# Small projections of the front half on column groups of TensorE, summed and turned by products with an identity

## The reference, cut to what matters

```python
uc = modulate(xc, norm_pre_mix[l], csh1, csc1) @ w_in[l]     # context tokens
u  = modulate(x,  norm_pre_mix[l], sh1,  sc1)  @ w_in[l]     # latent tokens
...
ba = u[..., GDN_CONV_CH + GDN_V:]        # 32 columns: beta and g of the first mixer
beta = jax.nn.sigmoid(ba[:2])
g = -jnp.exp(A_log)[:, None, :, None] * jax.nn.softplus(ba[2:] + dt_bias[:, None, :, None])
...
dt_raw = u[..., SSD_CONV_CH + SSD_INNER:]   # 16 columns: dt of the second mixer
dt = jax.nn.softplus(dt_raw + dt_bias.reshape(2, 1, G, Hg, 1))
```

## Time and profile before

| | us |
|---|---|
| median of 3 runs | 1415.59 |
| lowest and highest | 1414.0, 1417.88 |
| the profiled execution's own time | 1415.84 |
| its span | 1414.0 |
| TensorE busy | 1259.0 (89%) |
| VectorE busy | 485.5 (34%) |
| ScalarE busy | 254.6 (18%) |
| moved by DMA | 458.59 MB, 324 GB/s on average |

### The profile page before, as it was taken

How to read it: one execution, slowest core, us unless ns; L and a number is a source line. 1 busy time by engine, 2 the same in 40 slices (tenths; PEclk the granted TensorE clock), 3 DMA queues, 4 the chain that set the end, 5 groups by cost and what they waited for, 6 DMA issues and landing times.

```text
span 1414.0 us, 25289 instructions
## 1 busy us (share of the span) xinstructions
PE 1259.0 (89%) x10245; PEld 576.8 (41%) x10246; DVE 485.5 (34%) x1026; ACT 254.6 (18%) x494; POOL 122.9 (9%) x169
## 2 busy tenths in 40 slices
PE   5999898657997999998889988887999999999995
PEld 2545355556754334333333333332333334333432
DVE  1155369735767213221232212311223213212223
ACT  2321442235122111111111111000000100100101
POOL 0201460164300000000000000000000000000000
PEclk8999999658997999999999999998999999999998
DMA  9859111010494999999999999999999699969993
GB/s 355 330 169 360 35 60 44 4 33 4 136 346 184 425 429 425 427 426 428 427 426 428 425 428 426 427 426 426 427 427 420 264 426 428 426 266 428 427 427 145
DMA packets 48134, 458.59 MB, mean 324 GB/s; under 512 B 4416, under 2 KB 4816, under 8 KB 22736
## 3 DMA queue, kind: packets, MB, share of 16 engines
q1 hardware_dynamic: 48080, 457.81, 78.3%
HBM read 456.15 MB, written 1.05 MB: 323 GB/s over the span
## 4 chain that ended last, share of the span: by engine, by line
PE 59%; DMA 30%; DVE 5%; issue 3%; ACT 2%; POOL 1%; DVEq 0%; SPq 0%; ACTq 0%; POOLq 0%
DMA arena<-in_w_up 29%; PE bank L1154 22%; PE bank L1183 9%; PE bank L667 7%; PE bank L1125 3%; PE bank L1116 2%; PE bank L583 2%; PE bank L1047 2%; PE bank L543 2%; DVE arena L1726 1%; ACT arena L1541 1%; PE bank L592 1%; DMA arena<-in_x 1%; PE bank L1147 1%; PE bank L896 1%
## 5 line engine op out<-in xcount | busy, mean ns | idle before, releaser
L1154 PE MATMUL bank<-arena 128*64 128x512 f32 x2176 | 482.0, 596 | 35.2 <-DMA arena<-in_w_up 19.6
L1154 PEld LDWEIGHTS bank<-arena 128*64 128x64 f32 x2176 | 155.3, 136 | 342.9 <-issue 267.0
L1183 PE MATMUL bank<-arena 128*64 128x512 f32 x1088 | 239.4, 592 | 0.0
L2253 DVE TENSOR_SCALAR arena<-bank 128x512 f32<-128x512 f32 x34 | 23.6, 693 | 392.7 <-PE bank L1154 392.7
L1183 PEld LDWEIGHTS bank<-arena 128*64 128x64 f32 x1088 | 78.9, 136 | 137.7 <-issue 135.4
L667 PE MATMUL bank<-arena 128*128 128x512 f32 (+1 forms) x320 | 125.2, 545 | 0.0
L2234 DVE TENSOR_TENSOR arena<-arena,bank 128x512 f32<-128x512 f32 x140 | 86.7, 683 | 6.0 <-PE bank L1125 6.0
L667 PEld LDWEIGHTS bank<-arena 128*128 128x128 f32 x320 | 61.4, 196 | 59.0 <-issue 56.0
L1116 PEld LDWEIGHTS bank<-arena 128*128 128x128 bf16 x1680 | 60.2, 118 | 27.0 <-DVE arena L2257 25.8
L1125 PE MATMUL bank<-arena 64*128 64x512 f32 x280 | 69.6, 614 | 0.9 <-ACT arena L1543 0.9
L1543 ACT ACTIVATE arena<-bank 128x512 f32<-128x512 f32 x34 | 20.3, 598 | 253.2 <-PE bank L1183 253.2
(11 more groups left out here) (346 smaller groups left out, 1081.8 us busy)
## 6 DMA issues: line engine op xcount, KB each, us to landing
arena<-in_w_gate SPq DMA_DIRECT2D x64, 2048.0 KB, 20.3
arena<-in_w_up SPq DMA_DIRECT2D x64, 2048.0 KB, 21.9
arena<-in_w_down SPq DMA_DIRECT2D x64, 2048.0 KB, 20.6
arena<-in_w_ada SPq DMA_DIRECT2D x12, 2048.0 KB, 9.6
arena<-in_wfm SPq DMA_DIRECT2D x20, 512.0 KB, 3.4
arena<-in_wz SPq DMA_DIRECT2D x4, 1024.0 KB, 13.8
arena<-in_w_out SPq DMA_DIRECT2D x2, 2048.0 KB, 8.9
arena<-in_x SPq DMA_DIRECT2D x2, 1024.0 KB, 7.6
```

The lines of the kernel that those rows point to most:

```text
L1154: last = mm(ps[m][64 * c_:64 * c_ + 64, :], xcT[:, k, :], ring[:, 2 * h_ + m, k % 4, 512 * c_:512 * c_ + 512], start=False, stop=(k == KT ...
L1183: last = mm(ps[2][64 * c_:64 * c_ + 64, :], hidT[:, k % 4, 64 * (k // 4):64 * (k // 4) + 64], ring[:, 4 + h_, k % 4, 512 * c_:512 * c_ + 5 ...
L2253: v.tensor_scalar(hid[:, 0], ps[0][:, :], LIMIT, None, ALU.min).then_inc(*L.mark("a"))
```

## The change

The six `small_of` calls go. In their place stand two pieces.

`small_products()`, in one place behind `z_of(1, 1, 1)`, makes the weights the stationary operand. Part 0 takes 32 of the 48 columns over tokens 0 to 511, part 1 takes columns 16 to 47 over the context and the permuted latent tokens. Feature block `k` stands in column group `k % 4`, so a bank (2 for part 0, 3 for part 1) holds four partial sums with the weight columns on the partitions and 512 tokens in the row. ScalarE copies each bank to `smT`, which lies where `xh` was.

`small_sums()`, behind `fm(0)`, takes 128 tokens of `smT` as the stationary operand and `eye32` (an identity of 32 stacked four times over the partitions) as the moving one. One product sums the four groups and turns the result to tokens on partitions. `eye32` is made by GpSimd, as before.

`cumulate()` moves from behind `fm(1)` to behind `fm(2)`, and VectorE's reading of it from block 1 to block 2.

```diff
+        smT = view(area("xh"), 2, 512)
...
-            def small_of(t, lo, hi):
-
-                base = t * 128 if lo == 0 else 512 + (t - 2) * 128
-                for k in range(KT):
-                    last = mm(smp[:, t, lo:hi], xmT[:, k, base:base + 128], wsmt[:, k, lo:hi],
-                              start=(k == 0), stop=(k == KT - 1))
+            def small_products():
+
+                pe.wait_ge(*L.at("in", "wsm", 1))
+                for t in range(2):
+                    pe.wait_ge(*L.at("act", "xmT", t))
+                    pe.wait_ge(*L.at("dve", "xmT", t))
+                for part in range(2):
+                    for k in range(KT):
+                        g = k % 4
+                        dst = view(ps[2 + part][32 * g:32 * g + 32, :], 2, 256)
+                        tokens = xmT[:, k, 0:768].rearrange("p (a b) -> p a b", a=3)[:, 0:3:2, :] if part else view(xmT[:, k, 0:512], 2, 256)
+                        last = mm(dst, wsmt[:, k, 16 * part:16 * part + 32], tokens, start=k < 4, stop=k >= 4)
+                    last.then_inc(*L.mark("smT", part))
+
+            def small_sums():
+
+                pe.wait_ge(*L.at("pool", "eye32"))
+                pe.wait_ge(*L.at("act", "smT", 1))
+                for t in range(NT):
+                    mm(smp[:, t, 0:32], smT[:, 0, 128 * t:128 * t + 128], eye32, start=True, stop=True)
+                    last = mm(smp[:, t, 32:48], smT[:, 1, 128 * t:128 * t + 128], eye32[:, 16:32], start=True, stop=True)
                 last.then_inc(*L.mark("sm"))
...
             z_of(0, 1, 1)
             rows_turned(0)
-            pe.wait_ge(*L.at("in", "wsm", 1))
-            small_of(2, 0, 32)
             z_of(1, 0, 1)
             rows_turned(1)
-            small_of(3, 0, 32)
-            pe.wait_ge(*L.at("act", "xmT", 0))
-            pe.wait_ge(*L.at("dve", "xmT", 0))
-            small_of(0, 0, 48)
             z_of(1, 1, 1)
-            pe.wait_ge(*L.at("act", "xmT", 1))
-            pe.wait_ge(*L.at("dve", "xmT", 1))
-            small_of(1, 0, 48)
-            small_of(2, 32, 48)
-            small_of(3, 32, 48)
+            small_products()
...
                 if i < NFM:
                     fm(i)
-                if i == 1:
+                if i == 0:
+                    small_sums()
+                if i == 2:
                     cumulate()
...
             z_out(1, 1)
+            for part in range(2):
+                act.wait_ge(*L.at("pe", "smT", part))
+                f(smT[:, part], ps[2 + part][:, :], ACT.Copy).then_inc(*L.mark("smT", part))
...
-                if i == 1:
+                if i == 2:
                     dve.wait_ge(*L.at("pe", "cum"))
```

## The result

| | before | after |
|---|---|---|
| median of four runs | 1416.74 us (1414.0 to 1419.05) | 1400.99 us (1398.16 to 1402.47) |
| profiled execution | 1415.84 us, span 1414.0 | 1402.24 us, span 1400.4 |
| granted clock of TensorE | 0.954 | 0.960 |

The two profiled executions differ by 13.6 us, of which the forecast covers 6.6. The question is where the other 7 us come from.

What follows compares the result with a forecast made beforehand. The prediction took TensorE alone to bound the front, from 55.95 us to the `row` product. 10.48 + 1.70 - 3.71 - 0.15 - 1.71 = 6.6 us off 1415.84 gave 1409.2 us, range 1405.8 to 1413.3.

Steps and rivals of the forecast that it cites:

- The small products, 3.71 us: Ahead of `fm(0)`: the 16 added column-group products take 2 x 1.855 = 3.71 us, by the `ada_chunk` row.
- The sums, 1.71: Behind `fm(0)`: the eight added products of `small_sums` take 1.71 us, with ScalarE's second copy to `smT` hidden.
- Leaving the groups, 0.15: At `fm(0)`, now behind column groups: leaving them adds 0.15 us, as for `fm(2)` behind an `ada_chunk`.
- Full overlap: In `small_products`: four column groups overlap as in `ada_chunk`, eight products in 1.86 us (3.8 times).
- Side engines, cover 0.2 us: At the `row` product: VectorE's `mod` is ready at 94.0 us, the product due at 94.2, leaving 0.2 us.
- rival (b): At the `row` product: it waits for VectorE's `mod`, stretched convolutions costing 0.5 or 1.1 us; 1410.3 us, chance 0.10.
- The clock, 1.70 us: First two `fm` blocks: without the narrow products TensorE's clock no longer falls, so 1.70 us come back.
- Rival (a): Around `fm`: the clock gain isn't had, as it falls anyway or not all earlier runs fell; 1.70 us, 1410.9, chance 0.14.
- Every microsecond taken from TensorE there moves all that follows: From 55.95 us to the `row` product: the chain is TensorE alone, so savings carry through unless another engine becomes late.
- the result line 1415.84 - 6.6: Whole kernel: the profiled execution's 1415.84 us less the front's 6.6 us gives 1409.2 us.
- Rival (c): Beyond the front: the gain is given back at a stage started by something not moved; 1415.6 us, chance 0.07.

Runs made afterwards that it cites:

- the kernel before at place 0: Kernel before plus 161 semaphore increments on TensorE that nothing waits for, spread over the `fm` products: 1410.51 us, ratio 0.9981 against the kernel before.
- the changed kernel at place 95: Changed kernel plus 95 semaphore increments on TensorE that nothing waits for, spread over the `fm` products: 1405.86 us, ratio 0.9951 against the kernel before.
- two later measurements: Changed kernel word for word, 1402.27 us, and with 256 semaphore increments more on TensorE, 1402.93 us; ratios 0.9909 and 0.9928 against the kernel before.
- its repeat: Changed kernel measured once more, word for word, against more runs of the kernel before: 1402.27 us, ratio 0.9909.
- the sums early: Changed kernel with `small_sums` directly behind `small_products`, ahead of `fm(0)`: 1411.41 us in one run.
- the changed kernel with 32 fillers: Changed kernel plus 32 semaphore increments on TensorE that nothing waits for, spread over the `fm` products: median 1406.24 us, ratio 0.9945 against the kernel before.
- the kernel before with its narrow products apart: Kernel before with the last two `small_of` calls (16 columns) moved behind `fm(0)` and `cumulate` behind `fm(2)`: 1422.66 us in one run.

## Why the prediction was wrong, by its steps

- **The small products, 3.71 us**: 3.57. **The sums, 1.71**: 1.69, with ScalarE's copy hidden. **Leaving the groups, 0.15**: the block behind `small_products` takes 7.07 us, one behind the sums 6.96. The z products, which the prediction left at 3.52 and 3.51, took 3.44 each.
- **Full overlap**: 3.9 times, measured. The rule that was set against it (the Trainium skill, TensorE: Matmul & The Clock Gate, Part 3, three groups at 0.79 of the ideal), taken over to four groups, doesn't hold for these products.
- **Side engines, cover 0.2 us**: a wait of 0.24 us at the `row` product, by the slow first step of the second convolution, which overlaps a GpSimd product that starts at 89.55 us: a small form of rival (b), within the profile's 6.61 us. That the front gave 6.61 us to the hundredth is luck in part: this wait was made up by the z products and the 0.14 us of the small ones.
- **The clock, 1.70 us**: the mechanism was right, and the size was right for the execution it was read from. The prediction took the 3.51 us and 4.38 us stretches as harmless because one execution had passed them; two other executions fell behind such a stretch. Rival (a) feared that not all runs have the fall; all four profiles with this order of narrow products have one, and one of them has two. How much more than 1.70 us that makes on average is not shown.
- **"Every microsecond taken from TensorE there moves all that follows"**, and the result line 1415.84 - 6.6: this is the step that failed. It takes the later stages as fixed in length. They depend on where TensorE's breaks fall, and the change shifts those by 95 instructions. Worth about 3 us: the first stretch takes 22.4 to 23.4 us at the old place and 18.6 to 20.9 at the new one, in both kernels, and the medians say 2.6 (the kernel before at place 0) and 3.8 to 4.7 (the changed kernel at place 95). Rival (c) asked only whether something gives the gain back, never whether something adds to it.
- **The size that was measured**: 6.6 and 3 are 9.6 us, and the two later measurements gave 11.1 and 12.0, each uncertain by some 4 us; both of their medians are still below the range. The 15.8 us of the first had four runs of either kernel, of kernels whose single runs spread over 18 (before) and 11 to 15 us (changed). Even the 1415.84 us that the forecast started from is some 2 us above the medians of the kernel before in the later comparisons. In the first pair of profiles the 7 us beyond the front are 3.8 of the first stretch (23.44 against 19.62), less the 1.3 of the later start; most of the rest, 2.7 us, lies between 323 and 350 us of the kernel before, where the other executions don't follow the place. The spread sits between the load of `x` and that of `w_out`: 65.1 us in the changed kernel's profile and 71.1 in its repeat, where the granted clock from 280 to 350 us was 0.79 and 0.70. The repeat has some 24 us on end at the low clock there; three of the other 14 profiles have the like (the sums early, the changed kernel with 32 fillers, and the kernel before with its narrow products apart; 1411.41, 1413.47 and 1422.66 us). So it comes with either front. These are the two rows:

```profile
280.00:350.00 70.00, 51.22 (x2032) 44.85 (x2027) 34.01 (x65) 34.06 (x96) 48.84 (x50) 0.79 0.08 23
```

```profile
280.00:350.00 70.00, 51.74 (x1818) 43.57 (x1815) 30.18 (x58) 31.17 (x91) 46.52 (x47) 0.70 0.05 18
```

Open are three things: what a break is, since only its period and its effect were measured; what brings on the long low clock between 330 and 375 us in some executions; and what brings the clock down behind one narrow stretch of 3.5 us and not behind the next.

## What to carry to other kernels

Replace products that stream few columns by products in column groups: here that saves the work and, with it, clock falls of which one profile may show only a part. If a change alters the number of TensorE's instructions, expect stretches of tiny products far behind it to change by a few microseconds either way, and measure the change at equal places (with fillers up to the next 256) before crediting it with the whole difference. Where the times spread too much to tell, compare the length of the same stretch over several profiles: here that showed the 3 us which the medians left in doubt. Where single runs spread over 15 us, a forecast's range must include the spread of a median of four.

## What the runs showed of the hardware

TensorE pauses for 1.0 to 2.7 us at multiples of 256 of its instructions where these are tiny products without a pause between them, and the medians of the same kernel with its places moved over a period of 256 differ by 6.5 to 7.5 us. The pauses fit a fetch of instructions: the Trainium skill, Runtime: NRT & Kernel Launch, Instruction fetch mechanics, has them fetched in blocks of 256. It also says that the fetch is hidden, because instructions are issued more slowly than they are fetched; if the pauses are fetches, this trace disagrees for this form of code, by the 2.43 us ahead of 252.72 and its like. That the pause is the fetch itself was not tested, only that it moves with the count.

The granted clock falls to its lower level behind products of 16 to 48 streamed columns while TensorE is busy without a gap (2.00 of 2.00 us in the earlier trace rows, 6.00 of 6.00 above), which costs 1.7 us each time (5.20 against 3.51 us, 5.27 against 3.57, 8.80 against 7.10). The 3.57 us of products in column groups were followed by the full clock in every profile of the changed kernel that had no narrow products ahead of them.
